# Output projection by tokens as seven half-size products, with the second norm taken from row sums

## The reference, cut to what matters

```python
...
    mod = c_silu @ w_ada + b_ada
    sh1, sc1, ga1, sh2, sc2, ga2 = jnp.split(mod[:, None, :], N_MOD, axis=-1)
...
    return (g_a * (y_a @ w_proj_a) + g_b * (y_b @ w_proj_b)) @ w_out      # merge_branches
...
    x = x + ga1 * merge_branches(y_a, y_b, gate_logits, w_proj_a, w_proj_b, b_gate, w_out)
    h2 = modulate(x, g_ffn, sh2, sc2)        # rms_norm(x, g) * (1 + scale) + shift
    x = x + ga2 * conv_ffn(h2, w_up, conv_w, conv_b, w_down, rows, GRID_W)
...
    return rms_norm(x, g_final)
```

## Time and profile before

| | |
|---|---|
| Median of 3 runs | 477.36 us (476.3 to 477.41) |
| Profiled execution: its own time | 475.77 us |
| Its span, first to last instruction | 473.8 us |
| TensorE busy | 454.1 us, 96% of the span |
| VectorE busy | 390.7 us, 82% |
| ScalarE busy | 105.1 us, 22% |
| GpSimd busy | 46.2 us, 10% |
| Mean granted TensorE clock | 0.994 of full speed |
| HBM read | 93.91 MB |

### The profile page before, as it was taken

One profiled execution on the slowest core, in us unless ns is written; L12 is line 12 of the kernel. 1 busy time (PEld: TensorE's weight loads), 2 busy tenths in 40 slices (PEclk: granted clock), 3 DMA queues, 4 the chain that ended last, 5 costly groups with the idle time before them and its releaser, 6 DMA issues.

```text
span 473.8 us, 7779 instructions
## 1 busy us (share of the span) xinstructions
PE 454.1 (96%) x2670; PEld 346.6 (73%) x2670; DVE 390.7 (82%) x821; ACT 105.1 (22%) x194; POOL 46.2 (10%) x76
## 2 busy tenths in 40 slices
PE   4899999999999899989999999999999999999995
PEld 2444457899888788878878888887888887444454
DVE  3799999999999967961064999998999999899654
ACT  5422455143122134000142211111111011200002
POOL 2100110004030313000000110110110111000000
PEclk9999999999999999999999999999999999999999
DMA  7993499635999999952999533543443443100002
GB/s 295 424 418 133 142 338 143 234 145 99 112 323 414 362 408 372 395 180 89 397 404 396 180 120 147 177 158 109 177 155 117 171 177 123 54 0 1 0 0 89
DMA packets 21930, 96.87 MB, mean 204 GB/s; under 512 B 6480, under 2 KB 7120, under 8 KB 13200
## 3 DMA queue, kind: packets, MB, share of 16 engines
q1 hardware_dynamic: 15024, 74.70, 44.4%
q0 software_dynamic: 5488, 20.19, 13.4%
q10 hardware_dynamic: 1392, 1.63, 1.0%
HBM read 93.91 MB, written 2.59 MB: 204 GB/s over the span
## 4 chain that ended last, share of the span: by engine, by line
PE 89%; DVE 6%; issue 1%; DMA 1%; ACT 1%; DVEq 0%; ACTq 0%
PE bank L694 31%; PE bank L705 14%; PE bank L502 12%; PE bank L659 6%; PE bank L610 6%; PE bank L426 3%; PE bank L477 3%; PE bank L462 3%; DVE s_region L948 2%; PE bank L491 2%; PE bank L450 1%; PE bank L591 1%; PE bank L628 1%; DMA a_raw<-s5raw 1%; PE bank L366 1%
## 5 line engine op out<-in xcount | busy, mean ns | idle before, releaser
L694 PE MATMUL bank<-h_all,s_region 128*128 128x256 f32 x704 | 152.4, 379 | 0.7 <-ACT ctx_region L897 0.7
L694 PEld LDWEIGHTS bank<-h_all,s_region 128*128 128x128 f32 x704 | 133.6, 190 | 19.2 <-ACT ctx_region L897 1.1
L1383 DVE SCALAR_TENSOR_TENSOR ctx_region<-ctx_region,pk_sb 128x189 f32<-128x189 f32 (+2 forms) x352 | 127.4, 437 | 0.1
L502 PE MATMUL bank<-h_all,ring_region 128*128 128x256 f32 x256 | 57.8, 388 | 0.0
L502 PEld LDWEIGHTS bank<-h_all,ring_region 128*128 128x128 f32 x256 | 49.5, 195 | 7.5 <-issue 0.6
L705 PE MATMUL bank<-s_region,ring_region 128*128 128x512 f32 (+1 forms) x132 | 47.6, 521 | 0.0
L705 PEld LDWEIGHTS bank<-s_region,ring_region 128*128 128x128 f32 x132 | 25.1, 190 | 22.6 <-issue 21.5
L897 ACT ACTIVATE ctx_region<-bank 128x512 f32<-128x512 f32 x22 | 13.1, 597 | 124.7 <-PE bank L694 68.2
L948 DVE TENSOR_TENSOR s_region<-s_region,power 128x2048 f32<-128x2048 f32 (+1 forms) x16 | 38.1, 2420 | 0.1
L1298 DVE SCALAR_TENSOR_TENSOR s_region<-s_region 128x1024 f32<-128x1024 f32 x28 | 33.3, 1222 | 1.4 <-DMA s_region<-mod_w 0.9
L426 PE MATMUL bank<-h_all,ring_region 128*128 128x512 f32 x64 | 31.1, 614 | 2.6 <-ACT h_all L774 2.6
(11 more groups left out here) (212 smaller groups left out, 466.8 us busy)
## 6 DMA issues: line engine op xcount, KB each, us to landing
s_region<-up_w SPq DMA_DIRECT2D x33, 1024.0 KB, 4.8
ring_region<-ring_w SPq DMA_DIRECT2D x26, 1024.0 KB, 7.5
s_region<-mod_w POOLq DMA_DIRECT2D x28, 512.0 KB, 7.9
s_region<-early_w SPq DMA_DIRECT2D x4, 1024.0 KB, 21.8
gates<-early_w SPq DMA_DIRECT2D x2, 1024.0 KB, 10.7
s_region<-k_scratch POOLq DMA_DIRECT2D x8, 256.0 KB, 12.1
x_region<-x_t SPq DMA_DIRECT2D x1, 1024.0 KB, 4.9
ctx_region<-ctx_t SPq DMA_DIRECT2D x1, 1024.0 KB, 7.2
```

Of the source, the lines that this page charges most:

```text
L502: mx = pe.matmul(bank[5 - j % 2][:, mm * TOK:(mm + 1) * TOK], ring[:, u % RING, (mm * KD + k) * P:(mm * KD + k + 1) * P], h_x[:, k, :], st ...
L694: mx = pe.matmul(bank[s % 3][:, half * TOK:(half + 1) * TOK], up_ring[:, s, (half * KD + k) * P:(half * KD + k + 1) * P], h2[:, k, :], sta ...
L1383: dve.scalar_tensor_tensor(out=o, in0=a, scalar=cw[:, tile[half], (dy + 1) * 3 + dx + 1], in1=o, op0=ALU.mult, op1=ALU.add).then_inc(s_con ...
```

## The change

The output projection becomes one of tokens by features. `merged` is cut into halves by token (h) and by even and odd feature tile (k), `w_out` into halves by output feature (f) and by even and odd tile; each product of two halves is four matmuls of 128x512 (one of the seven, with the minus sign, is done as two parts of 256 columns, called 4 and 8). VectorE makes four arrays from `merged` (`out_s`, and one in place) and four from the weights (`out_t1` and three in place, 128x2048 each). Results are collected by VectorE, scaled by `ga1` spread over all partitions (`ga1_bc`), and added to `x1_tok`, which is now loaded by token (`x_tok`).

`w_out` is no longer in the ring. It has a place of its own in `up_ring` slots 4 to 7 and is issued by SyncE right behind unit 18 (`U_PROJ + 1`), once `s_y8_ps` is 2 (the last L591 record of PE). The rows units become 21 and 22. The up-projection's slots 0 to 3 and 8 to 10 are issued once sum 27 is done, slots 4 to 7 after the last product. `ga1` is added up after sum 11, stored to HBM feature by feature by GpSimd ahead of `mod_w` tile 20, and read back on all partitions after tile 27.

The squares go to ScalarE with `accum_out`, the root and the reciprocal are of one column, VectorE scales the rows (`x_hat`, 128x1024 twice), and TensorE transposes these; ScalarE writes `h2` from PSUM.

```diff
-U_OUT = U_PROJ + 4
-U_ROWS = U_OUT + 4
+U_ROWS = U_PROJ + 4
 UNITS = U_ROWS + 2
...
+        w_out = s5_region[:, 4 * UNIT:8 * UNIT].rearrange("p (i k f n) -> p i k f n", i=KD // 2, k=2, f=2)
+        out_t1 = x_region[:, :].rearrange("p (i n) -> p i n", i=KD // 2)
+        x_hat = x_region[:, :].rearrange("p (h n) -> p h n", h=2)
+        merged_pair = merged.rearrange("p (i k) (h t) -> p i k h t", k=2, h=2)
+        out_s = [gate_region[:, i * 512:(i + 1) * 512].rearrange("p (i t) -> p i t", i=KD // 2) for i in range(3)]
+        out_sums = [ctx_region[:, i * 512:(i + 1) * 512] for i in range(4)]
+        ga1_bc = u_x[:, :].rearrange("p (f n) -> p f n", f=2)
         merge_tmp = sb("merge_tmp", 2 * TOK)[:, :].rearrange("p (b t) -> p b t", b=2)
...
-            full = UNITS // RING
+            full = U_GLU // RING
...
+                if u == U_PROJ + 1:
+                    sp.wait_ge(s_y8_ps, 2)
+                    for i in range(KD // 2):
+                        sp.dma_start(up_ring[:, 4 + i, :], out_w[i]).then_inc(s_wo[i], 16)
             sp.wait_ge(s_mt_used, MT)
-            for s in range(USLOTS):
+            for s in (0, 1, 2, 3, 8, 9, 10):
+                sp.dma_start(up_ring[:, s, :], up_w[s]).then_inc(s_up[s], 16)
+            sp.wait_ge(s_po, 8)
+            for s in range(4, 8):
                 sp.dma_start(up_ring[:, s, :], up_w[s]).then_inc(s_up[s], 16)
             with sp.Fori(1, UP_ROUNDS + 1) as r:
                 for s in range(USLOTS):
@@ -342,11 +365,17 @@
...
                 if t == 20:
                     pool.wait_ge(s_y8_ps, 2)
-                    pool.dma_start(x_region[:, :], x_t).then_inc(s_xr, 16)
+                    pool.dma_start(x1_tok.rearrange("p h f n -> p (h f n)"), x_tok).then_inc(s_xr, 16)
+                    pool.wait_ge(s_ga1, 1)
+                    pool.dma_start(ga1_dram[:].rearrange("a (k p) -> p (a k)", p=P), mod2[:, 0:KD], allow_slow_non_contiguous=True).then_inc(s_ga1_out, 16)
                 if t >= MTS:
                     pool.wait_ge(s_mt_used, t - MTS + 1)
                 pool.dma_start(mod_tile[t % MTS], mod_w[t]).then_inc(s_mt[t % MTS], 16)
-            pool.wait_ge(s_unit, U_OUT + 3)
+            pool.wait_ge(s_ga1_out, 16)
+            pool.wait_ge(s_ya, KS)
+            pool.wait_ge(s_unit, U_GLU + 1)
+            pool.dma_start(ga1_bc.rearrange("p f n -> p (f n)"), ga1_dram[:].partition_broadcast(P)).then_inc(s_ga1_row, 16)
+            pool.wait_ge(s_unit, U_PROJ + 3)
...
+            def out_product(n, lhs, rhs, cols=slice(0, 512)):
+                for i in range(KD // 2):
+                    if n == 1:
+                        pe.wait_ge(s_wo[i], 16)
+                        pe.wait_ge(s_mg, 2 * i + 1)
+                    mx = pe.matmul(bank[OUT_BANK[n]][:, cols], lhs(i), rhs(i)[:, cols], start=(i == 0 and n not in (2, 3)), stop=(i == KD // 2 - 1),
+                                   skip_group_check=True)
+                mx.then_inc(s_po, 1)
+
+            out_product(1, lambda i: merged_pair[:, i, 0, 0, :], lambda i: w_out[:, i, 0, 0, :])
+            pe.wait_ge(s_to, 1)
+            pe.wait_ge(s_so, 1)
+            out_product(5, lambda i: out_s[0][:, i, :], lambda i: out_t1[:, i, :])
+            pe.wait_ge(s_pc, 1)
+            out_product(2, lambda i: merged_pair[:, i, 1, 0, :], lambda i: w_out[:, i, 1, 0, :])
+            pe.wait_ge(s_so, 2)
+            pe.wait_ge(s_pc, 2)
+            out_product(3, lambda i: out_s[2][:, i, :], lambda i: w_out[:, i, 1, 1, :])
+            pe.wait_ge(s_to, 2)
+            out_product(6, lambda i: out_s[1][:, i, :], lambda i: w_out[:, i, 0, 0, :])
+            pe.wait_ge(s_so, 3)
+            pe.wait_ge(s_to, 3)
+            out_product(7, lambda i: merged_pair[:, i, 0, 1, :], lambda i: w_out[:, i, 0, 1, :])
+            pe.wait_ge(s_to, 4)
+            for half in range(2):
+                out_product((4, 8)[half], lambda i: merged_pair[:, i, 1, 1, :], lambda i: w_out[:, i, 1, 0, :], slice(half * 256, half * 256 + 256))
+
+            def x_hat_transposed(h, b):
+
+                for k in (2 * b, 2 * b + 1):
+                    mx = pe.transpose(bank[XHAT_BANK[b]][:, (k % 2) * TOK + h * P:(k % 2) * TOK + (h + 1) * P], x_hat[:, h, k * P:(k + 1) * P], ident[:, :])
+                mx.then_inc(s_xhat_tr, 1)
 
             later_rows(U_ROWS)
-            pe.wait_ge(s_x1, KD)
-            x1_transposed(4, 0, 0)
+            pe.wait_ge(s_xhat, 1)
+            for b in range(KD // 2):
+                x_hat_transposed(0, b)
             later_pick(0)
             later_rows(U_ROWS + 1)
-            x1_transposed(5, 0, 4)
             later_pick(1)
-            x1_transposed(7, 1, 0)
...
+            for i, n in enumerate((1, 5)):
+                act.wait_ge(s_po, i + 1)
+                act.activation(out_sums[i], bank[OUT_BANK[n]][:, :], ACT.Copy).then_inc(s_pc, 1)
+
+            def row_squares(n, src, width):
+
+                act.wait_ge(s_x1, n + 1)
+                if n > 0:
+                    act.wait_ge(s_row2, n)
+                act.activation(square_out[:, 0:width], src, ACT.Square, accum_out=row2_sum[:, n:n + 1]).then_inc(s_row2, 1)
+
+            def row_root(h, last):
+
+                act.wait_ge(s_row2, last + 1)
+                act.wait_ge(s_eps2, h + 1)
+                act.activation(row2_std[:, h:h + 1], row2_sum[:, last:last + 1], ACT.Sqrt, scale=1.0 / D, bias=row2_bias[:, h:h + 1]).then_inc(s_std2, 1)
+
+            row_squares(0, x1_tok[:, 0, 0, :], 512)
+            row_squares(1, x1_tok[:, 0, 1, :], 512)
+            row_root(0, 1)
+            row_squares(2, x1_tok[:, 1, 1, :], 512)
+            for half in range(2):
+                row_squares(3 + half, x1_tok[:, 1, 0, half * 256:half * 256 + 256], 256)
+            row_root(1, 4)
...
+            dve.wait_ge(s_mt_used, 12)
+            dve.tensor_tensor(mod2[:, 0:KD], mod_sum[:, 0:KD], par("b_ada")[:, 2 * KD:3 * KD], ALU.add).then_inc(s_ga1, 1)
...
-                modulation_sums(20 + m, 21 + m)
+                if m < 6:
+                    modulation_sums(20 + m, 21 + m)
+                elif m == 6:
+                    for i in range(KD // 2):
+                        dve.wait_ge(s_wo[i], 16)
+                    dve.tensor_tensor(out_t1, wo12, wo11, ALU.subtract).then_inc(s_to, 1)
+
+
+            m11, m12, m21, m22 = merged_pair[:, :, 0, 0, :], merged_pair[:, :, 1, 0, :], merged_pair[:, :, 0, 1, :], merged_pair[:, :, 1, 1, :]
+            dve.tensor_tensor(out_s[0], m21, m22, ALU.add).then_inc(s_so, 1)
+            dve.wait_ge(s_so, 1)
+            tt(out_s[1], out_s[0], m11, ALU.subtract)
+            settle()
+            dve.tensor_tensor(out_s[2], m12, out_s[1], ALU.subtract).then_inc(s_so, 1)
+            dve.tensor_tensor(m21, m11, m21, ALU.subtract).then_inc(s_so, 1)
+            modulation_sums(26, 28)
+            dve.wait_ge(s_po, 1)
+            dve.wait_ge(s_to, 1)
+            dve.tensor_tensor(wo11, wo22, out_t1, ALU.subtract).then_inc(s_to, 1)
+            dve.tensor_tensor(wo12, wo22, wo12, ALU.subtract).then_inc(s_to, 1)
 
             dve.wait_ge(s_mt_used, MT)
-            dve.tensor_tensor(mod2[:, 0:MT], mod_sum[:, :], par("b_ada")[:, 2 * KD:2 * KD + MT], ALU.add).then_inc(s_mod2, 1)
...
+            dve.wait_ge(s_po, 3)
+            dve.wait_ge(s_to, 2)
+            dve.tensor_tensor(wo21, wo11, wo21, ALU.subtract).then_inc(s_to, 1)
...
+            def residual(b, h, f, src, cols=slice(0, 512)):
+
+                tt(scaled_out[:, b, cols], src, ga1_bc[:, f, cols], ALU.mult)
+                settle()
+                dve.tensor_tensor(x1_tok[:, h, f, cols], x1_tok[:, h, f, cols], scaled_out[:, b, cols], ALU.add).then_inc(s_x1, 1)
+
+            def row_bias(h, of, into, plus):
+
+                dve.tensor_scalar(row2_bias[:, into:into + 1], row2_sum[:, of:of + 1], 1.0 / D, plus, ALU.mult, ALU.add).then_inc(s_eps2, 1)
+
+            def normed_rows(h):
+
+                dve.wait_ge(s_std2, h + 1)
+                mark(dve.reciprocal(row2_std[:, h:h + 1], row2_std[:, h:h + 1]))
+                settle()
+                dve.tensor_scalar(x_hat[:, h, :], x1_tok[:, h].rearrange("p f n -> p (f n)"), row2_std[:, h:h + 1], None, ALU.mult).then_inc(s_xhat, 1)
+
             dve.wait_ge(s_xr, 16)
-            for m in range(KD):
-                dve.wait_ge(s_unit, U_OUT + m // 2 + 1)
-                dve.scalar_tensor_tensor(out=x_sb[:, m, :], in0=bank[OUT_BANK[m // 2]][:, (m % 2) * TOK:(m % 2 + 1) * TOK], scalar=mod2[:, m:m + 1],
-                                         in1=x_sb[:, m, :], op0=ALU.mult, op1=ALU.add).then_inc(s_x1, 1)
-            dve.wait_ge(s_x1, KD)
-            dve.wait_ge(s_std, 2)
-            mark(dve.reciprocal(rstd[:, 0:TOK], rstd[:, 0:TOK]))
-            settle()
-            for k in range(KD):
-                dve.tensor_tensor(h2[:, k, :], x_sb[:, k, :], rstd[:, 0:TOK], ALU.mult).then_inc(s_norm2, 1)
+            dve.wait_ge(s_ga1_row, 16)
```

(83 more changed lines are left out.)

35 lines of the change are left out of this document (14 added, 21 removed).

## The result

The changed kernel takes 486.77 us (median; 484.25 to 487.15), the kernel before 477.38: a ratio of 1.0198, with a 95% interval of 1.017 to 1.0225. It is 9.4 us slower where 2.9 were forecast. The direction and the first mechanism were as forecast; the size was not, and the time lies above the range (to 485.5).

What follows compares the result with a forecast made beforehand. The prediction took TensorE, busy 96% of the span, to bound the kernel. Its terms, -5.0 (stage) + 6.9 (transfer) + 1.0 (store), gave +2.9 us, 480.3 us on the median, range 475.5 to 485.5.

Steps and rivals of the forecast that it cites:

- the first mechanism: Loading out_w early delays the mod_w tiles, so VectorE's y_a and TensorE's second half of the branch projection come late.
- Part 1, the products: Output projection on TensorE: seven products take 24.0 us, back to back, with VectorE's operands ready in time.
- Part 2, from the last product to the up-projection: VectorE and ScalarE are the path; branch projection's end to up-projection takes 33.3 us instead of 38.3, 5.0 gained.
- The wait behind ScalarE's root: TensorE's picks wait for ScalarE's modulation-row copies behind the root; root ends T+29.2, transposes T+33.1 (T: branch projection's end).
- Part 3, the transfer: out_w's early load delays mod_w tiles and y_a, starting the second half of the branch projection 6.9 us late.
- the two thirds: out_w in SyncE's queue takes two thirds of DMA bytes, slowing GpSimd's mod_w to one tile in 3.8 us.
- The tail of 2.1 us: Time from a mod_w tile's last byte to the start of VectorE's sum: 2.1 us, lower bound 0.6.
- Part 4, the store: Storing ga1 as 1024 pieces of 4 bytes ahead of tile 20 adds 1.0 us to the path, bounds 0 to 3.
- The estimate of 5.2 us: The ga1 store's time if reading, modifying and writing small pieces doubled each piece, instead of 2.6 us.
- the transfer is hidden: Rival: mod_w keeps its pace against out_w, nothing waits and the 5.0 us gain remains, 472.4 us; chance 0.15.
- Near cancellation: Rival: tail of 0.6, no store loss and a 5.5 gain give -0.8 to +1.4 us, 476.6 to 478.7; chance 0.15.
- The store that stalls the merge loop: Rival: ga1's store at double price, or longer VectorE and ScalarE hand-overs, gives 483.3 us and above; chance 0.15.

Runs made afterwards that it cites:

- run 9: Changed kernel, out_w halves behind units 19 and 20, x_tok behind tile 27, ga1 stored as 8 rows of 512 bytes, modulation-row copies ahead of ScalarE's root: 472.0 us.
- run 12: Kernel of run 1 with seven matmuls of ones filling TensorE's gap ahead of the first pick of the modulation rows: 480.04 us.
- run 1: Changed kernel with ga1 stored as 128 pieces of 32 bytes instead of 1024 of 4, its values in another order: 482.24 us.
- run 4: Kernel before the change, with 4 MB of unused data loaded where the change loads out_w: 485.2 us.
- run 10: Kernel of run 1 with twenty matmuls of ones filling TensorE's gap before the second half of the branch projection: 482.41 us.
- run 5: Kernel before the change, with an unused store of 1024 pieces of 4 bytes ahead of tile 20: 483.99 us.

## Why the prediction was wrong in size

Two terms of the sum failed: the store, which was put at 1.0 us and measured 4.5, and TensorE's clock behind a wait, which was put at nothing and measured 2.3 us in one place and 2.6 in another. By the forecast's own sum, either alone would have left the time inside the range (an estimated 483.8 and 485.2 on the median).

**Part 1, the products: right.** 24.0 us were forecast, 24.05 measured in run 9 and in run 12. In the changed kernel itself they wait, but only because VectorE is late with the merged tiles; in run 1, with no late tile, they do not.

**Part 2, from the last product to the up-projection: right but for the clock.** 33.3 us forecast; 32.6 in run 12, 34.7 in run 1. The wait behind ScalarE's root was there: TensorE stood 2.6 us before the first pick in run 1. What was missed is that this gap brings the clock down and that the steps behind it (pick, second rows unit, pick, eight transposes) then cost 5.6 us and not 3.0. Run 12 shows it, with 2.2 us. The rest of the part was counted 1.2 us too long, most of it in VectorE's steps, and this hid half of the miss. (0.2157, given as 22.46 / 104, is 0.216; nothing in the sum moves by it.)

**Part 3, the transfer: right.** `y_a` was forecast to end at 194.3 to 195.0 and ended at 194.77 in run 1 and 193.67 in the changed kernel; the two thirds held, and so did one tile in 3.8 us: sums 15 and 16 of run 1 start at 182.44 and 186.18. The tail of 2.1 us fits, but no run shows it by itself. Against before, the second half starts 5.65 us late in the changed kernel, 6.75 in run 1 and 7.9 in run 4, so the forecast's 6.9 is right to about a microsecond. But the term counts only the wait; for the clock behind it the prediction had no term, though a gap of 6 us was in it. That adds 2.3 us (22.98 against 20.7 in run 1; 20.72 with the gap filled, run 10).

**Part 4, the store: the term that failed most.** I took 1.0 us, bounds 0 and 3, from the row of 256-byte pieces, 2.6 us of the engines. It holds them down for some 8 us, and its share of the time is 4.5 us (changed kernel against run 1), 6.8 in the kernel before (run 5). The row was far: those pieces were 256 bytes, went into on-chip memory and not out to HBM, and were in q1. The price was also passed to the path too lightly: tile 20 was 3.4 us later than counted, waits before the next sums came on top, and the first sum of `merged` ended 7.3 us behind the branch projection, not 2.0 (224.22 and 216.93). Which of the three differences makes the piece dear, the runs don't separate. Nor do they say whether it is the size or the number: at 0.13 us a piece and 8 pieces an engine, the store of run 1 would be an estimated 1 us.

The Trainium skill, "DMA: Bandwidth & Descriptors", Specifications, says that pieces under 512 bytes are read, modified and written. The estimate of 5.2 us made from it in the prediction was too low as well. The runs agree in that such a store is dear (some 8 us, run 5); none shows that reading and writing back is the reason.

**The sum again.** -5.0 + 6.9 was +1.9 without the store. In run 1 the up-projection starts 5.4 us later than before (252.52 against 247.09). The difference of 3.5 is the clock, 2.3 us at the second half of the branch projection and 2.6 at the end of part 2, less 1.2 by which part 2 was otherwise shorter than counted, and less 0.2 by which `y_a` came sooner. By the medians run 1 is 5.0 slower than before, and the changed kernel 4.5 slower than run 1.

**The rivals.** That the transfer is hidden is refuted by runs 4 and 1. Near cancellation would have needed the clock to hold and the store to cost nothing. The store that stalls the merge loop was the right rival: at 483.3 and above it named the mechanism and the side, and its chance of 0.15 was too small for a cost known only from a far row.
